# A fifth weight place for the first layer's experts, over constants that are loaded again for the second layer

## What is computed

```
hl, hc = modulated rmsnorm of xl (256 tokens) and xc (256 context tokens)
projections with w_in (1024 columns in, 1824 out); rotary turns; two kinds of attention; a short convolution
xl = xl + g1 * (mixed @ w_o)                       # layer 0: xc likewise
def ec_ffn(h, router_w, w_gate, w_up, w_down):     # 16 experts, each takes its 32 best tokens
    aff = softmax(h @ router_w); top_aff, idx = top_k(aff of each expert, 32)
    xg = h[idx]
    hid = silu(xg @ w_gate) * (xg @ w_up)          # w_gate, w_up: 1024 x 512 for each expert
    y = (hid @ w_down) * top_aff                   # w_down: 512 x 1024 for each expert
    return zeros.at[idx].add(y)
xl = xl + g2 * ec_ffn(...)                         # layer 0: xc likewise
```

## Time and profile before

| | before |
|---|---|
| median of 3 runs | 2254.77 us (2252.86 to 2255.13) |
| the profiled execution | 2254.89 us, its span 2253.1 us |
| PE busy | 2084.7 us (93%), 14083 matmul records |
| DVE, ACT, POOL busy | 930.5, 457.4, 86.6 us |
| read from memory | 432.23 MB, mean 192 GB/s over the span |
| mean granted clock of TensorE | 0.976 of full speed |
| layer 0's experts | from 383 to 612 us of the span |
| layer 1's experts | from 852 to 1059 us |

### The profile page before, as it was taken

How to read it: one execution, slowest core, us unless ns; L and a number is a source line. 1 busy time by engine, 2 the same in 40 slices (tenths; PEclk the granted TensorE clock), 3 DMA queues, 4 the chain that set the end, 5 groups by cost and what they waited for, 6 DMA issues and landing times.

```text
span 2253.1 us, 32562 instructions
## 1 busy us (share of the span) xinstructions
PE 2084.7 (93%) x14083; PEld 1614.4 (72%) x14083; DVE 930.5 (41%) x1861; ACT 457.4 (20%) x1008; POOL 86.6 (4%) x87
## 2 busy tenths in 40 slices
PE   6999999999899988666999999999999998999998
PEld 3444587655565467444878888899988788889998
DVE  2137723223335732112356423456615544145662
ACT  3004522111122421101133112100003321121001
POOL 1000010000000000000001100000000011000000
PEclk9999989999999999888999999999999999999999
DMA  9651603999922639999422314445643231244463
GB/s 368 239 188 47 224 1 154 404 426 423 413 105 75 224 141 425 428 427 415 146 81 107 113 38 150 150 150 163 156 150 131 94 113 48 102 150 151 168 159 85
DMA packets 172927, 435.36 MB, mean 193 GB/s; under 512 B 6218, under 2 KB 64498, under 8 KB 156146
## 3 DMA queue, kind: packets, MB, share of 16 engines
q1 hardware_dynamic: 171648, 430.90, 51.4%
q10 hardware_dynamic: 1138, 2.39, 0.3%
HBM read 432.23 MB, written 1.05 MB: 192 GB/s over the span
## 4 chain that ended last, share of the span: by engine, by line
PE 82%; DMA 10%; DVE 4%; ACT 2%; issue 1%; ACTq 0%; DVEq 0%
PE bank L273 78%; DMA arena<-in_exp_w_gate 3%; DMA arena<-in_exp_w_up 3%; PE bank L537 2%; PE bank L783 1%; DMA arena<-in_exp_w_down 1%; DMA ring<-in_exp_w_up 1%; DMA ring<-in_exp_w_gate 1%; DMA ring<-in_w_in 1%; DMA arena<-in_x 1%; DVE arena L732 0%; ACT arena L737 0%; ACT h L645 0%; ACT h L625 0%; PE bank L463 0%
## 5 line engine op out<-in xcount | busy, mean ns | idle before, releaser
L273 PE MATMUL bank<-h,ring 128*128 128x256 f32 (+3 forms) x3376 | 756.2, 383 | 12.6 <-ACT arena L591 4.9
L273 PEld LDWEIGHTS bank<-h,ring 128*128 128x128 f32 (+1 forms) x3376 | 598.3, 192 | 155.2 <-issue 77.1
L273 PE MATMUL bank<-arena 128*128 128x128 f32 (+11 forms) x3588 | 462.3, 333 | 50.4 <-DMA arena<-in_exp_w_gate 16.3
L273 PEld LDWEIGHTS bank<-arena 128*128 128x128 f32 (+5 forms) x3588 | 356.1, 178 | 137.7 <-issue 69.0
L273 PE MATMUL bank<-arena,ring 128*128 128x128 f32 (+1 forms) x1704 | 267.9, 317 | 1.0 <-PE bank L273 1.0
L273 PEld LDWEIGHTS bank<-arena,ring 128*128 128x128 f32 x1704 | 245.9, 191 | 19.6 <-PE bank L273 1.8
L737 ACT ACTIVATE arena<-bank 128x256 f32<-128x256 f32 (+5 forms) x263 | 116.0, 461 | 595.1 <-PE bank L273 569.7
L732 DVE COPY arena<-bank 128x256 f32<-128x256 f32 (+7 forms) x114 | 60.9, 536 | 266.6 <-PE bank L273 213.6
L273 PE MATMUL bank<-ring,arena 128*32 128x128 f32 (+1 forms) x1632 | 119.1, 336 | 20.5 <-DMA ring<-in_exp_w_up 11.0
L273 PEld LDWEIGHTS bank<-ring,arena 128*32 128x32 f32 (+1 forms) x1632 | 83.1, 126 | 60.5 <-DMA ring<-in_exp_w_gate 14.5
L273 PE MATMUL bank<-h,arena 128*128 128x128 f32 (+2 forms) x560 | 106.8, 331 | 4.3 <-ACT arena L1323 2.6
(11 more groups left out here) (339 smaller groups left out, 1695.4 us busy)
## 6 DMA issues: line engine op xcount, KB each, us to landing
ring<-in_w_in SPq DMA_DIRECT2D x31, 2048.0 KB, 7.9
ring<-in_exp_w_gate SPq DMA_DIRECT2D x19, 2048.0 KB, 12.2
ring<-in_exp_w_up SPq DMA_DIRECT2D x19, 2048.0 KB, 14.2
ring<-in_ada_w SPq DMA_DIRECT2D x18, 2048.0 KB, 10.3
ring<-in_exp_w_down SPq DMA_DIRECT2D x17, 2048.0 KB, 15.8
ring<-in_w_ffn_gate SPq DMA_DIRECT2D x10, 2048.0 KB, 8.0
ring<-in_w_ffn_up SPq DMA_DIRECT2D x10, 2048.0 KB, 7.8
arena<-in_exp_w_down SPq DMA_DIRECT2D x9, 2048.0 KB, 27.2
```

Source lines behind the costliest of these rows:

```text
L273: return PE.matmul(o, lhsT, rhs, start=(k == 0), stop=(k == n - 1))
```

## The change

Experts 1 to 15 of layer 0 may use `SPARE_SLOT` as a fifth place. It lies over `cst1` and over the parts of `uq` and `ukv` that belong to layer 1. To that end the arena is laid out anew: layer 1's parts stand directly behind `cst1` and layer 0's behind those, since the latter are scratch in layer 0's experts. Layer 1's parts are no longer loaded at the start. A new list `again_list` (the constants, and layer 1's `uq` and `ukv`) is loaded behind layer 1's fourth `w_in` matrix, once PE has used the last expert matrix that stood in the place. PE and DVE wait for it ahead of layer 1's `("in", 1)`.

```diff
@@ -235,10 +235,11 @@
         cst1 = arena[:, o:o + N_FIRST]
         o += N_FIRST
-        uq = arena[:, o:o + L * 1152].rearrange("p (l k n) -> p l k n", l=L, k=2)
-        o += L * 1152
-        ukv = arena[:, o:o + L * 768].rearrange("p (l n) -> p l n", l=L)
-        o += L * 768
+        uq, ukv = [None] * L, [None] * L
+        for l in reversed(range(L)):
+            uq[l] = arena[:, o:o + 1152].rearrange("p (k n) -> p k n", k=2)
+            ukv[l] = arena[:, o + 1152:o + 1920]
+            o += 1920
@@ -340,7 +341,7 @@
         def expert_homes(l, e):
 
-            return [*range(RING), CONST_SLOT, *(FREED if l == L - 1 and e else ())]
+            return [*range(RING), CONST_SLOT, *(FREED if l == L - 1 and e else (SPARE_SLOT,) if e else ())]
@@ -940,8 +941,7 @@
-            if l == 0:
-                pe.wait_ge(late_loaded, 16 * len(late_list))
+            pe.wait_ge(*((again_loaded, 16 * len(again_list)) if l else (late_loaded, 16 * len(late_list))))
             join(tensor, pe, ("in", l))
@@ -1049,8 +1049,7 @@
-            if l == 0:
-                dve.wait_ge(late_loaded, 16 * len(late_list))
+            dve.wait_ge(*((again_loaded, 16 * len(again_list)) if l else (late_loaded, 16 * len(late_list))))
             join(vector, dve, ("in", l))
@@ -2742,12 +2741,13 @@
         second_list = []
+        again_list = late_list[:]
         for l in range(L):
-            late_list += [
-                (uq[:, l], A["mla_w_uq"][l].rearrange("(k p) n -> p k n", p=P)),
-                (ukv[:, l], A["mla_w_ukv"][l]),
-                (rtr[:, l], A["router_w"][l].rearrange("(k p) n -> p k n", p=P)),
-            ]
+            (again_list if l else late_list).extend([
+                (uq[l], A["mla_w_uq"][l].rearrange("(k p) n -> p k n", p=P)),
+                (ukv[l], A["mla_w_ukv"][l]),
+            ])
+            late_list.append((rtr[:, l], A["router_w"][l].rearrange("(k p) n -> p k n", p=P)))
@@ -2766,6 +2766,8 @@
+        again_after = [max(m for m in range(last_expert[0] + 1) if home[m] == SPARE_SLOT)]
@@ -2839,9 +2841,10 @@
-                    if home[n] == STORE_SLOT or home[n] in FREED and fills[n] == 1:
+                    layer = int(n > last_expert[0])
+                    if home[n] == STORE_SLOT or home[n] in FREED and holder_before[n] in (None, *again_after):
                         for s in (tensor, scalar, vector):
-                            value = s.closed(("mixed", L - 1 if home[n] in FREED or fills[n] == L else 0))
+                            value = s.closed(("mixed", layer))
@@ -2851,6 +2854,10 @@
+                    if n == last_expert[0] + 4:
+                        wait_used(again_after[0])
+                        for dst, src in again_list:
+                            sp.dma_start(dst, src).then_inc(again_loaded, 16)
```

More of the change, by code:

```diff
@@ L210, in program @@
         loaded = [sem(f"slot_loaded_{i}") for i in range(RING + 6)]
-        const_loaded, cond_loaded, tokens_loaded, vec_loaded, rest_loaded, late_loaded, second_loaded, stored = (
-            sem(n) for n in ("const_loaded", "cond_loaded", "tokens_loaded", "vec_loaded", "rest_loaded", "late_loaded",
+        const_loaded, cond_loaded, tokens_loaded, vec_loaded, rest_loaded, late_loaded, again_loaded, second_loaded, stored = (
+            sem(n) for n in ("const_loaded", "cond_loaded", "tokens_loaded", "vec_loaded", "rest_loaded", "late_loaded", "again_loaded",
                              "second_loaded", "stored"))
@@ L963, in hybrid_tensor @@
                 for k in range(2):
-                    last = mm(b[0:96, 0:TQ], uq[:, l, k, 96 * i:96 * i + 96], cq[:, k, 0:TQ], k, 2)
+                    last = mm(b[0:96, 0:TQ], uq[l][:, k, 96 * i:96 * i + 96], cq[:, k, 0:TQ], k, 2)
                 last.then_inc(*tensor.mark("q96", l, i))
@@ L970, in hybrid_tensor @@
                 b = take(pe, "k96", l, i)
-                mm(b[LO, :], ukv[:, l, 128 * i:128 * i + 64], ckv[:, 0, :], 0, 1).then_inc(*tensor.mark("k96", l, i))
-            wv = ukv[:, l, :].rearrange("p (h a) -> p h a", a=P)[:, :, 64:128]
+                mm(b[LO, :], ukv[l][:, 128 * i:128 * i + 64], ckv[:, 0, :], 0, 1).then_inc(*tensor.mark("k96", l, i))
+            wv = ukv[l].rearrange("p (h a) -> p h a", a=P)[:, :, 64:128]
             for j in range(4):
```

2 lines of the change are left out of this document (1 added, 1 removed).

## The result

The changed kernel takes 2249.69 us, the median of 12 runs (2246.66 to 2251.41). The kernel before, on the same chip, takes 2254.95 us (12 runs, 2251.42 to 2258.37). The ratio is 0.9979 with an interval of [0.9971, 0.9986], so the change gains 3.2 to 6.5 us. Two later comparisons of the same kernel gave 0.9985 [0.9976, 0.9993] and 0.9982 [0.9973, 0.9992].

A forecast was written before the change was run, and what follows sets the result against it. The kernel was taken as mostly PE-bound, with transfers limiting PE late in layer 0's experts. The further place's −5.0 us and zero for the other terms took 2254.77 to 2249.8 us, range 2247.4 to 2252.8.

The forecast's parts named there:

- The term of the further place, −5.0 us: Layer 0's experts: a fifth place lands each matrix one transfer earlier, −5.0 us; bounds 4.9 and 6.7 us.
- 1.7 us of waiting left, none before expert 14: Layer 0's experts: PE's waits for weights fall from 6.7 to about 1.7 us, all in experts 14 and 15.
- DMA engines at the same times, each matrix one transfer earlier: Layer 0's experts: DMA engines work at the same times as before, but each matrix lands 5.03 us earlier.
- The scatter at 608.5: PE's scatter after layer 0's expert 15 was to begin at 608.5 us instead of 613.52.
- What follows layer 0's experts, 0: From layer 0's experts through layer 1's experts, everything moves 5.0 us earlier and gives nothing back: term 0.
- The reload, 0: Constants and layer 1's two matrices, reloaded during layer 1's projections, land 73 us before first use: term 0.
- What leaves the start, 0 to −0.4: At the start, layer 1's 960 KB, 2.3 us of transfer, no longer load: 0, at most −0.4 us.
- the rival of a smaller gain: Whole kernel: all ways to a gain below 4.5 us, or none, clock losses among them; chance 0.34.
- PE's own pace: Layer 0's experts: two or three PE clock losses leave 3.3 or 1.6 us of gain; inside the 0.34.
- the place brings nothing: Layer 0's experts: the new load comes only at 387 or DMA was already busy, 2254.8 us; chance 0.03.
- the reload is late: Layer 1 before its attention waits for the constants, 1 us per us landed after 699.3; slower, chance 0.04.
- all of the waiting goes: Layer 0's experts: transfers gain more, PE loses all 6.7 us of waits, 2248.1 us; chance 0.10.

The follow-up runs named there:

- three places: The kernel before without the place over the second block's constants for layer 0's experts 1 to 15; 2264.76 us, ratio 1.005.
- swapped place: The changed kernel with the new place replacing the one over the second block's constants in layer 0, so four places, reload kept; 2254.26 us, ratio 1.0001.
- reload alone: The changed kernel with the four old places in layer 0; new layout, smaller load at the start and reload stay; 2253.84 us, ratio 1.0003.
- reload late: The changed kernel with the reload issued four matrices later, behind the fourth `ada_w` matrix; 2262.26 us, ratio 1.0039.
- layer 0 early: The changed kernel with gate of expert 1 in layer 0 issued as soon as attention is done; 2250.18 us, ratio 0.9983.
- layer 1 early: The changed kernel with gate and down of layer 1's expert 1 issued once attention is done; 2248.49 us, ratio 0.9973, and again 2248.92 us, ratio 0.998.
- from expert 2 on: The changed kernel with the fifth place used from expert 2 on only, no fourth matrix at the start; 2249.7 us, ratio 0.998.
- the place used once: The changed kernel with the fifth place taking gate of expert 1 only, four places afterwards; 2255.04 us, ratio 1.0002.
- the first four experiments: First four told: fifth place for one matrix only (2255.04 us), from expert 2 on (2249.7), three places (2264.76), swapped place (2254.26).

## Why the prediction was right, point by point

**What bounds the stretch.** Right: PE follows the transfers from the middle of the experts on. Taking a place away cost 11.7 us in the measure, giving one gained 5.6, and where PE stands at the end it waits 1.22 us ahead of an up matrix with five places as with four.

**The term of the further place, −5.0 us.** The mechanism holds and the size was slightly small. The measure by number of places:

| places in layer 0 | kernels | us from first release to up of expert 15 | mean |
|---|---|---|---|
| 3 | three places | 226.6 | 226.6 |
| 4 | before, swapped place, reload alone | 215.0, 214.6, 215.15 | 214.9 |
| 5 | changed three times, reload late, layer 0 early, layer 1 early twice | 208.8, 209.4, 209.1, 210.0, 209.3, 209.15, 209.4 | 209.3 |

The difference is 5.6 us, where I had 45.23 / 9 = 5.03 for one transfer. It lies between the bounds −4.9 and −6.7 that stood there. What the working had one-sided is where the gain comes from: it derived the term from the idle stretch before the first release alone, but five places that leave this stretch empty (from expert 2 on) already bring 3.5 us, out of the holes that follow it. As to what fills the 0.6: when the queue is steady, landings come 4.93 us apart, so one transfer is if anything less than 5.03. The rest must come out of the holes in the landings, of which the table of landings shows a shorter one for five places after the fourth (5.8 and 5.0 us against 6.3 and 5.8). But single steps of 5.4 to 6.4 us turn up in other spots of every trace, and two of the three traces with four places have 5.5 and 5.3 us for the first of these steps and 4.9 for the second, and so, with three and seven traces, I can't tell a systematic part from them. That stays open.

The waits of PE don't add up to 6.2 us by themselves: 6.7 − 1.5 is 5.2. Each row of up matmuls that starts without a wait begins 3.45 us ahead of the next row, and one that is followed by a wait lasts 3.67. So a wait costs some 0.2 us more than its idle time, and there are 5 fewer (2 for 7). That is about 1 us, and 5.2 + 1 accounts for the 6.2.

**1.7 us of waiting left, none before expert 14.** Right: 1.5 us, the first at 579.69, which is up of expert 14. **Issues at the start.** Right: four in 1.4 us, then none until 385.63. **DMA engines at the same times, each matrix one transfer earlier.** Right, by the first two lines of the landings.

**The scatter at 608.5.** It came at 605.82. Of the 2.7 us by which that is off, 1.5 are the earlier start of the experts in this execution, which is no part of the change, and 1.2 are what the middle piece of this trace has over the 5.0 of the term.

**What follows layer 0's experts, 0.** Right: from up of expert 15 to the transposes of L948 it was 102.22 us and is 102.25. Layer 1's experts took 209.16 us from gather to up of expert 15 (842.59 to 1051.75) and take 209.20.

**The reload, 0.** Right, and with nearly the lead that I had worked out. The issues of the reload and their landings in the changed kernel, KB and us from issue to landing:

```profile
arena<-consts SPq DMA_DIRECT2D x1, 1136.0 KB, 15.3
...
arena<-in_mla_w_ukv SPq DMA_DIRECT2D x1, 384.0 KB, 13.3
```

The last lands at 610.96 + 13.3 = 624.3 us; PE's first row to need it is at 696.68 and waits for VectorE. That is 72 us early, where 73 were predicted. SP was held in the issue of the constants for 4.37 us, which is within the 6 that I had allowed; nothing stood behind it until 642.02.

**What leaves the start, 0 to −0.4.** Not separable. The first release falls between 385.43 and 387.31 in eleven kernels with the reload (mean 386.5), and at 387.10 and 386.95 in two without. A gain of 0.5 us would be in keeping with that, and so would none.

**The sum.** −5.0 to the profile's own time gave 2249.9, and 2249.01 was measured. In that execution −6.2 and −1.5 were partly offset by +1.8 behind the experts. So the mechanism and its term are right, but that the median of 2249.69 lies within 0.1 us of the 2249.8 on record is luck: the gains of the same two kernels in three comparisons are up to 1.3 us apart. By the ratios these gains are 4.7, 3.4 and 4.1 us, so two of them lie below the 4.5 us that I had set as the edge of the forecast, where the rival of a smaller gain begins. All three lie below the stretch's own 5.6 us, which is inside the intervals of the first and the third (up to 6.5 and 6.1 us: 0.9971, 0.9973) and just outside that of the second (0.9976, 5.4 us). The traces show no place where the change would give a part back: from up of expert 15 to the end of the span it is 1650.9 to 1654.5 us in the three traces with four places of the table (mean 1652.3), and 1649.9 to 1652.8 in four with five places (changed three times and layer 0 early, mean 1652.0). Whether the missing 1 to 2 us are more than chance stays open.

**The rivals.** Of PE's own pace: the one loss that was there came again (2.36 us of idle time ahead of 475.69, then 5.00 us for 16 matmuls, as 5.35 in the earlier trace rows), no second one, and five places still leave 1.5 us of waits. That the place brings nothing is refuted, that the reload is late too. That all of the waiting goes is refuted for the place as built.

## What to carry to other kernels

Where a consumer follows a stream of transfers, count the places, and look for idle DMA time just ahead of the stretch: where the places already keep the queue filled, one more, kept in the rotation to the end, is worth about one transfer once (5.6 us here), and not one per round; where they don't, it is worth more (11.7 us from three to four). Loading a matrix earlier into a place that exists anyway brings nothing if all of them have landed by the time the first place is released, as in layer 0. Where transfers are still under way at that moment, as in layer 1, it can bring a little. Data that stands in such a place can be reloaded for nothing if the reload is issued as soon as its place is free and lands before the first use; look at what the issuing queue does behind it, since each us too late costs one.

## What the runs showed of the hardware

**A transfer alone is far slower than one in a row.** 2048 KB issued into an empty queue landed after 7.5 to 8.1 us at layer 0's first release in every trace (8.9 and 9.0 us at layer 1's in the two traces with layer 1 early), and behind others 4.93 us after the one before. The Trainium skill, "SBUF — State Buffer", section "The DMA setup-cost knee", gives a fit of 2 us + bytes / 436 GB/s, which makes an estimated 6.8 us for one, and 4.8 us for its part without the 2 us; the runs show 0.7 to 1.3 us more for a single one (2.1 and 2.2 in those two traces), and agree in the steady pace to about 0.1 us. What I had not expected is how early the next issue must be for the 2.7 us to be hidden. A transfer issued 1.3 us before the landing ahead of it (399.39 against 400.7, before) landed 6.5 us after that, one that came 1.5 us too late (402.81 against 401.3, the place used once) 9.2 us after, and a few us of lead still left 5.8 us at times. That is roughly 7.7 us from its own issue or 4.9 us from the landing ahead, whichever is later. It is a fit to these few steps and no rule: the 8.9 and 9.0 us in layer 1, and steps of up to 6.4 us with 4 to 6 us of lead in the kernel with three places, lie above it.

**Issues can hold SP.** The rows of SP above show 3.78 and 1.64 us for two `w_in` matrices and 4.37 us for the constants, issued while transfers are under way. An expert matrix of 2048 KB mostly takes 0.3 to 0.5 us, and the constants took 0.58 (at 698.62) in the kernel with the late reload, where only one matrix was in the queue ahead of them. No experiment was made to vary this.

**The clock of PE differs between executions in the same rows.** In the second block 16 matmuls took 3.72 us in the profile of before, and in the one of after, where the granted clock from 1320 to 1340 us is 0.83 instead of 0.95:

```profile
1330.01 3.72 PE L273 MATMUL bank<-h,ring 128*128 128x256 f32 x16 [0.47 <-ACT arena L737]
```

```profile
1322.42 5.39 PE L274 MATMUL bank<-h,ring 128*128 128x256 f32 x16 [0.47 <-ACT arena L738]
```

Likewise 32 matmuls of layer 1's gather took 9.48 us before (842.59) and 7.99 after (835.00), though the two rows wait alike. 0.83 is a mean over the two levels, 1.2 and 2.4 GHz. The gather's granted clock was 0.82 in the one and 1.00 in the other. Each such place is worth 1.5 to 1.7 us either way. It fits this that the stretch of layer 0 keeps within 0.7 us of its mean in seven traces while whole runs spread over some 3 us either way, and that slower runs tend to have a lower mean clock: of the kernel before, beside the first four experiments, the fastest run had 2249.35 us at 0.980 and the slowest 2258.04 us at 0.975. That these places make up the whole spread is not shown.
